# Attention stage of a hybrid decoder layer: dividing by the row sums before the transposes, short blocks in a second PSUM place, a new order in the unit, mean squares token-major

## What is computed

```python
logits = jnp.einsum('bqhd,bkhd->bhqk', q_blk, k) * scale + (c_q[..., :, None] - c_k[:, :, None, :])
p = jax.nn.softmax(jnp.where(causal, logits, -jnp.inf), axis=-1)
return jnp.einsum('bhqk,bkhd->bqhd', p, v)
...
mix = jnp.concatenate([_rmsnorm(rec, rec_out_norm_w[l]), _rmsnorm(att, attn_out_norm_w[l])], axis=-1)
x = x + jnp.einsum('bse,ed->bsd', mix, w_out[l])
```

## Time and profile before

| what | value |
|---|---|
| median of 3 runs | 2045.23 us (2040.22 to 2046.78) |
| the profiled execution | 2041.34 us, of which the span is 2039.6 us |
| PE busy | 1899.4 us (93% of the span) |
| DVE busy | 1277.3 us (63%) |
| ACT busy | 1050.6 us (52%) |
| stage B, first score work to last norm work | about 284 to 450 us of the span |
| stage C | 450.3 to about 568 us |

### The profile page before, as it was taken

One profiled execution on the slowest core, in us unless ns is written; L12 is line 12 of the kernel. 1 busy time (PEld: TensorE's weight loads), 2 busy tenths in 40 slices (PEclk: granted clock), 3 DMA queues, 4 the chain that ended last, 5 costly groups with the idle time before them and its releaser, 6 DMA issues.

```text
span 2039.6 us, 51127 instructions
## 1 busy us (share of the span) xinstructions
PE 1899.4 (93%) x20629; PEld 1761.9 (86%) x20629; DVE 1277.3 (63%) x2642; ACT 1050.6 (52%) x1442; POOL 402.3 (20%) x302
## 2 busy tenths in 40 slices
PE   6999988979968999999999999999999999989982
PEld 4777756658858999999999999999999999988982
DVE  4543647764378555566665567776677687776681
ACT  5574335552105444455555556555665665655661
POOL 4010000001002111111111112213243243333241
PEclk9999999989968999999999999999999999999996
DMA  4111010015377788889999899999999999999994
GB/s 141 52 42 42 21 62 1 2 46 189 137 260 246 262 280 280 272 274 304 306 306 306 303 310 312 312 327 336 371 354 372 371 353 371 370 351 369 369 346 114
DMA packets 251771, 501.81 MB, mean 246 GB/s; under 512 B 13025, under 2 KB 33809, under 8 KB 251585
## 3 DMA queue, kind: packets, MB, share of 16 engines
q1 hardware_dynamic: 231376, 446.73, 60.4%
q0 software_dynamic: 20256, 51.73, 11.7%
q10 hardware_dynamic: 48, 2.10, 0.3%
HBM read 471.16 MB, written 52.43 MB: 257 GB/s over the span
## 4 chain that ended last, share of the span: by engine, by line
PE 54%; DVE 4%; DMA 4%; issue 4%; SPq 2%; ACT 1%; POOL 0%; DVEq 0%; ACTq 0%; POOLq 0%
PE E_p_d L1945 22%; PE E_p_g L1934 5%; PE E_p_g L1937 5%; PE E_p_g L1936 5%; PE E_p_u L1937 5%; PE E_p_u L1934 5%; PE E_p_u L1936 5%; DMA E_w_st<-in_w_down 4%; DVE E_w_lo L1775 3%; SPq L1570 2%; PE E_p_t L1916 2%; PE E_p_t L1901 2%; ACT E_w_hi L1689 1%; DVE E_up L1835 0%; DVE E_gate L1823 0%
## 5 line engine op out<-in xcount | busy, mean ns | idle before, releaser
L1775 DVE SCALAR_TENSOR_TENSOR E_w_lo<-E_w_st,E_w_hi 128x2048 f16<-128x2048 f32 x260 | 594.8, 2288 | 60.3 <-ACT E_w_hi L1689 56.6
L1689 ACT ACTIVATE E_w_hi<-E_w_st 128x2048 f16<-128x2048 f32 x260 | 493.0, 1906 | 142.4 <-PE E_p_g L1937 95.7
L1945 PE MATMUL E_p_d<-E_a_f,E_w_st 128*128 128x160 f32 (+6 forms) x4096 | 536.3, 291 | 21.7 <-DMA E_w_st<-in_w_down 13.4
L1945 PEld LDWEIGHTS E_p_d<-E_a_f,E_w_st 128*128 128x128 f32 x4096 | 521.2, 193 | 29.2 <-DMA E_w_st<-in_w_down 16.2
L1934 PE MATMUL E_p_g<-E_x_hi,E_w_hi 128*128 128x160 f16 (+6 forms) x2048 | 373.0, 224 | 7.2 <-DVE E_w_lo L1775 7.2
L1934 PE MATMUL E_p_u<-E_x_hi,E_w_hi 128*128 128x160 f16 (+6 forms) x2048 | 371.7, 223 | 5.0 <-DVE E_w_lo L1775 5.0
L1936 PE MATMUL E_p_g<-E_x_lo,E_w_hi 128*128 128x160 f16 (+6 forms) x2048 | 373.0, 224 | 0.0
L1937 PE MATMUL E_p_g<-E_x_hi,E_w_lo 128*128 128x160 f16 (+6 forms) x2048 | 372.9, 224 | 0.0
L1937 PE MATMUL E_p_u<-E_x_hi,E_w_lo 128*128 128x160 f16 (+6 forms) x2048 | 371.6, 223 | 0.0
L1936 PE MATMUL E_p_u<-E_x_lo,E_w_hi 128*128 128x160 f16 (+6 forms) x2048 | 371.6, 223 | 0.0
L1633 POOL DMA_INDIRECT sum_rows<-E_y_rows,E_idx_out x66 | 169.0, 2561 | 596.6 <-ACT E_y_rows L1707 586.4
(11 more groups left out here) (375 smaller groups left out, 2758.7 us busy)
## 6 DMA issues: line engine op xcount, KB each, us to landing
E_w_st<-in_w_gate_up SPq DMA_DIRECT2D x130, 2048.0 KB, 15.7
E_w_st<-in_w_down SPq DMA_DIRECT2D x64, 2048.0 KB
A_w_st<-in_w_in SPq DMA_DIRECT2D x20, 512.0 KB, 3.9
sum_rows<-C_x SPq DMA_DIRECT2D x10, 512.0 KB, 5.8
A_x_rows<-in_x SPq DMA_DIRECT2D x8, 512.0 KB, 8.2
...
```

The lines of the kernel that those rows point to most:

```text
L1689: act.activation(w_hi[c % RI][:], staged(c % NG), ACT.Copy, scale=SW).then_inc(hi_s, 1)
L1775: dve.scalar_tensor_tensor(out=w_lo[c % RI][:], in0=staged(c % NG), scalar=SW, in1=w_hi[c % RI][:], op0=ALU.mult, op1=ALU.subtract, accum_ ...
L1945: ins = pe.matmul(banks[:, h, 0:w], staged(c)[:, k, h * P:(h + 1) * P], x[:, k, 0:w], start=h == 0 and k == 0, stop=k == KT - 1, skip_grou ...
```

## The change

Stage B: once two exponentials' sums are there, DVE takes two reciprocals (`inverse(n)`), and the score tile itself is scaled before it is turned (`normal`): tile n on DVE, tiles n+1, n+2 and n+3 on ACT. The spreading matmuls and the multiplication of `out_rows` are gone. Tiles n+2 and n+3 are turned into `p_o[1]` instead of `p_t`. PE's order becomes: wide scores, turn n, weigh(u-1, short), turn n+2, turn n+1, slim scores, turn n+3, (sums), weigh(u, long). ACT and DVE keep their tiles in an order that fits. `sums` now has the squares as the fixed operand and one column of ones as the moving one, so that the means stand one per partition; eight matmuls of one column, written to two columns of `p_s[0]`. The reciprocal of all means is taken once, over 128x8.

Stage C: the root is taken of 128x8 after the second of the four splits of rec; eight matmuls between `rec_part(0)` and `rec_part(1)` spread it over the partitions into PSUM, and DVE's scaling reads it there.

```diff
+        def home_of(n):
+            return p_o[1] if n % 4 >= 2 else p_t
...
             def turn(n):
-                pe.wait_ge(exp_s, n + 1)
+                if n % 4:
+                    pe.wait_ge(norm_act, 3 * (n // 4) + n % 4)
                 else:
+                    pe.wait_ge(norm_dve, n // 4 + 1)
+                u, e = n // 4, n % 4
+                if e == 0 and u:
+                    pe.wait_ge(turn_dve, 2 * u - 1)
+                elif e == 1:
+                    pe.wait_ge(turn_act, 2 * u + 1)
+                elif e == 2 and u:
+                    pe.wait_ge(turn_dve, 2 * u)
+                elif e == 3:
+                    pe.wait_ge(turn_act, 2 * u + 2)
...
             def weigh(u, side):
-                pe.wait_ge(inv_s, u + 1)
-                if u:
-                    pe.wait_ge(out_s, 2 * u - 1 + side)
-                for e in range(2):
-                    pe.matmul(p_o[0][e * HD:(e + 1) * HD, o + P:o + 2 * P],
-                              row_inv[:, n + e:n + e + 1].to_broadcast([P, HD]), m.ident[:], start=True, stop=True)
+                if u or side:
+                    pe.wait_ge(out_s, 2 * u + side)
...
             def sums(q):
-                for c in range(CT):
-                    ins = pe.matmul(p_o[1][:, 0:2 * P], m.rec_ones[:], square[:, c, :], start=c == 0, stop=c == CT - 1)
+                for side in range(2):
+                    for c in range(CT):
+                        ins = pe.matmul(p_s[0][:, 512 + side:513 + side], square[:, c, side * P:(side + 1) * P],
+                                        m.rec_ones[:, 0:1], start=c == 0, stop=c == CT - 1, skip_group_check=True)
...
@@ tensor: body of unit u
                 if u:
                     weigh(u - 1, 1)
+                turn(n + 2)
                 turn(n + 1)
                 if u + 1 < NU:
                     score_pair(n + 6)
-                turn(n + 2)
-                weigh(u, 0)
                 turn(n + 3)
                 if u % 4 == 1 and u > 4:
                     sums(u // 4 - 1)
+                weigh(u, 0)
@@ scalar: body of unit u
+            def normal(n):
+                act.wait_ge(inv_s, 2 * (n // 4) + 1 + n % 4 // 2)
+                act.activation(tile_of(n)[:, 0:L], tile_of(n)[:, 0:L], ACT.Copy, scale=row_inv[:, n:n + 1]
+                               ).then_inc(norm_act, 1)
+                normal(n + 2)
+                normal(n + 3)
                 keep_turned(n)
+                keep_turned(n + 2)
                 if u + 1 < NU:
                     exps(n + 4)
                     exps(n + 5)
-                keep_turned(n + 2)
-                if u + 1 < NU:
                     exps(n + 6)
                     exps(n + 7)
+                    normal(n + 5)
@@ vector: body of unit u
-                inverse(u)
+                inverse(n + 2)
...
                     subtract(n + 6)
                     subtract(n + 7)
+                    inverse(n + 4)
+                    normal(n + 4)
+                keep_turned(n + 3)
+                if u % 4 == 1 and u > 4:
+                    mean(u // 4 - 1)
                 out_rows(u, 0)
-                keep_turned(n + 3)
...
+            dve.wait_ge(ms_s, T // 2)
+            step(dve.reciprocal(m.att_ms[:], m.att_ms[:]))
@@ stage C
-            act.activation(att_rs[:], m.att_ms[:], ACT.Sqrt).then_inc(att_ok, 1)
+                if g == 1:
+                    act.activation(att_rs[:], m.att_ms[:], ACT.Sqrt).then_inc(att_ok, 1)
...
             rec_part(0)
+            pe.wait_ge(att_ok, 1)
+            for t in range(T):
+                ins = pe.matmul(p_m[t // 4][:, t % 4 * P:(t % 4 + 1) * P], att_rs[:, t:t + 1].to_broadcast([P, P]), m.ident[:],
+                                start=True, stop=True)
+                if t % 4 == 3:
+                    ins.then_inc(rs_mm, 1)
```

More of the change, by code:

```diff
@@ L745, in rows_of, with out_at, turned_no @@
             return slice(i * P, (i + 1) * P)
+        def out_at(side):
+            return 2 * P * side
+        def home_of(n):
+            return p_o[1] if n % 4 >= 2 else p_t
+        def turned_no(n):
+            return n - n % 4 + (1, 3, 2, 4)[n % 4]
         BY_DVE = {0: 1, 4: 2, 6: 3}
@@ L783, in score_pair @@
                     pe.wait_ge(score_s, n)
+                u = n // 4
+                if n % 4 == 0 and u % 4 == 3 and u > 4:
+                    pe.wait_ge(ms_s, (u - 2) // 4)
                 for c0 in range(0, L, 512):
@@ L949, in keep_turned, with inverse, normal @@
                 L = P * (where(n)[0] + 1)
[L950 removed]
+                dve.wait_ge(turn_mm, turned_no(n))
                 if n >= 4:
                     dve.wait_ge(pv_mm, 2 * (n // 4) - 1 + n % 4 // 2)
[L953 to L957 removed]
+                dve.tensor_copy(turned_of(n)[:, 0:L], home_of(n)[:, 0:L]).then_inc(turn_dve, 1)
+            def inverse(n):
+                dve.wait_ge(exp_s, n + 2)
+                dve.reciprocal(row_inv[:, n:n + 2], m.row_sum[:, n:n + 2]).then_inc(inv_s, 1)
+            def normal(n):
+                L = P * (where(n)[0] + 1)
+                dve.wait_ge(inv_s, 2 * (n // 4) + 1)
+                dve.tensor_scalar(tile_of(n)[:, 0:L], tile_of(n)[:, 0:L], row_inv[:, n:n + 1], None,
+                                  ALU.mult).then_inc(norm_dve, 1)
             def out_rows(u, side):
[L960 removed]
+                o = out_at(side)
                 dve.wait_ge(pv_mm, 2 * u + 1 + side)
[L962 to L965 removed]
+                dve.tensor_copy(m.att[:, u % 4, rows_of(u // 4, side)], p_o[0][:, o:o + P]).then_inc(out_s, 1)
             def mean(q):
@@ L969, in mean @@
                 for side in range(2):
-                    ins = dve.tensor_scalar(m.att_ms[:, rows_of(q, side)], p_o[1][:, side * P:(side + 1) * P], EPS, None,
-                                            ALU.add)
+                    i = blocks[q][side]
+                    ins = dve.tensor_scalar(m.att_ms[:, i:i + 1], p_s[0][:, 512 + side:513 + side], EPS, None, ALU.add)
                 ins.then_inc(ms_s, 1)
-                dve.wait_ge(ms_s, q + 1)
-                for side in range(2):
-                    step(dve.reciprocal(m.att_ms[:, rows_of(q, side)], m.att_ms[:, rows_of(q, side)]))
             key_rows(0)
@@ L983, in _ @@
             key_rows(6)
+            inverse(0)
+            normal(0)
             for u in range(NU):
                 n = 4 * u
-                inverse(u)
+                inverse(n + 2)
                 if u + 1 < NU:
@@ L1002, in _ @@
                                       ALU.subtract).then_inc(wo_lo_s, 1)
-                if u % 4 == 1 and u > 4:
-                    mean(u // 4 - 1)
             out_rows(NU - 1, 1)
             mean(T // 2 - 1)
+            dve.wait_ge(ms_s, T // 2)
+            step(dve.reciprocal(m.att_ms[:], m.att_ms[:]))
 def stage_c(nc, m, a):
@@ L1133, in _ @@
                 dve.tensor_tensor(mix_lo[:, c, :], m.rec[:, c, :], f32(mix_hi[:, c, :]), ALU.subtract).then_inc(mix_lo_s, 1)
[L1134 removed]
             for half in range(2):
                 r = slice(half * 512, (half + 1) * 512)
+                dve.wait_ge(rs_mm, half + 1)
                 for c in range(CT):
                     dve.scalar_tensor_tensor(out=m.att[:, c, r], in0=m.att[:, c, r], scalar=att_w[:, c:c + 1],
[L1139 removed]
+                                             in1=p_m[half][:], op0=ALU.mult, op1=ALU.mult).then_inc(att_n, 1)
                 if half == 0:
```

43 lines of the change are left out of this document (15 added, 28 removed).

## The result

| | median | range | runs |
|---|---|---|---|
| before | 2044.31 us | 2040.22 to 2046.78 | 6 |
| changed | 2032.61 us | 2029.18 to 2035.38 | 6 |

The ratio is 0.9944, 95% interval 0.9930 to 0.9959: 11.7 us faster, between 8.4 and 14.3. The prediction was 2036.6 us, in a range of 2028 to 2044. The profiled execution took 2033.14 us (span 2031.4), 8.2 less than that of before.

A forecast was written before the change was run, and what follows sets the result against it. Stage B was taken to be paced by a ring of waits with no engine full, stage C's main part by PE. From 2045.2 us, -15.0 + 7.0 - 4.6 + 4.0 = -8.6 gave 2036.6 us, range 2028 to 2044.

The forecast's parts named there:

- The signs it named: Stage B and C: foretold body times, `wo_lo` waiting in bodies 3, 7, 11, last result about 10 us earlier.
- two signs that were to mean failure as a whole: PE's clock in the loop below 1.00, or divisions taking longer than the rows they are priced by.
- Term 1, the ring: Stage B loop: short turns move into waits and spreadings go, shortening the ring of waits; -15.0 us.
- Term 2, the divisions' side effects: Stage B: divisions make `wo_hi`, `wo_lo`, the second reciprocal and ACT's first copy late; +7.0 us.
- slower: the clock: Rival: PE's new stalls lower its clock in stage B's late bodies, 1.8 us each; ten give 2055; chance 0.07.
- Term 3, the tail: End of stage B: shorter last body, one multiply gone, reciprocals of 1.94 us become one of 128x8; -4.6 us.
- The sums between them I cost equal: End of stage B: the last sums, between final multiply and reciprocals, were to cost the same as before.
- Term 4, stage C: Start of stage C: root and spreading delay DVE's scaling, so `att_part(0)` comes 4.0 us late; +4.0 us.
- the upper end of the prediction: Start of stage C: cost of 6 us if PE's stalls keep the low clock longer.
- The sums' price: Stage B, bodies 5, 9, 13: sixteen records at 0.114 us each, 1.8 us in all.

The follow-up runs named there:

- e_best: The change with second reciprocal ahead of `wo_lo`, `wo_hi` ahead of the wide division, and stage C's spreading earlier; 2022.65 us, 0.9907 of the kernel before.
- e_ms: The kernel before with only the change's new mean squares, and stage C as in the change; 2039.60 us, 0.9983 of the kernel before.
- r_after: The change once more without an edit, also called the repeat; 2032.07 us, 0.9957 of the kernel before.
- e_both: The change with two edits: second reciprocal ahead of `wo_lo`, and `wo_hi` ahead of the wide division; 2026.05 us, 0.9922 of the kernel before.
- e_spread: The change with stage C's spreading moved earlier, after PE's second group of three matmuls of tile 0; 2026.45 us, 0.9927 of the kernel before.
- e_place2: The kernel before plus new mean squares, division first and second turning place, old order, `mean` ahead of `wo_lo`; 2040.39 us, 0.9989 of the kernel before.
- e_divboth: The kernel before plus new mean squares and division, one turning place, old order, reciprocal ahead of `wo_lo`, `wo_hi` ahead of wide division; 2031.98 us, 0.9958.
- e_hi: The change with ACT doing `wo_hi` ahead of the wide division; 2027.73 us, 0.9933 of the kernel before.

## Why the prediction was right

**The signs it named.** Body 2 took 8.16 us (8.5 foretold), body 6 7.51 (7.8), body 5 9.18 (9.4), body 8 9.00 (over 9), and `wo_lo` waited 1.2 to 1.3 in bodies 3, 7 and 11. The last result came 6.1 earlier, and 10.1 counted from the start of body 0 (10 foretold). But two signs that were to mean failure as a whole also came. PE's clock in the loop was below 1.00: 0.97 over the fourteen bodies, 0.99 in the repeat (the kernel before had 0.98 over its fourteen). And ACT's divisions took longer than their price, 1.14 us for 1024 columns and 0.39 for 128, for 1.04 and 0.3. The time came out in spite of both, since the low clock struck one or two bodies, and 0.1 us a division is small beside waits of a microsecond.

**Term 1, the ring (-15.0).** `e_best` is the change with the side effects out, `e_ms` supplies bodies 0 and 1 of the old loop at full clock. Between them: bodies 0 to 3 lose 0.80, 0.82, 0.90 and 0.89 (predicted 0.8 each); bodies 4 and 6 1.06 and 1.07 (1.0), body 7 0.32 (1.0, since `wo_lo` still stands there); bodies 8, 10, 11 together 2.2 (2.7); body 12 0.85 (0.3); bodies 5, 9, 13 together 4.5 (5.8). Sum 13.4. The links were right, and what looks missing in body 13 (0.7 for 1.8) is mostly what term 2 booked there for ACT's squares, 0.8. With the squares (0.6 and 0.8) the prediction had 13.6 for what is measured here. The timeline of the changed kernel, body 13:

```profile
411.97 1.13 ACT L915 ACTIVATE B_square<-att 128x512 f32<-128x512 f32 x2
...
413.76 0.66 PE L827 MATMUL B_p_o<-ident,B_slim 128*128 128x128 f32 x4 [0.23 <-ACT B_slim L900]
...
415.06 0.74 PE L827 MATMUL B_p_t<-ident,B_wide 128*128 128x128 f32 x5 [0.63 <-ACT B_probs_t L908]
...
417.35 1.84 PE L851 MATMUL B_p_s<-rec_ones,B_square 128*128 128x1 f32 x16
```

PE waits 0.86 us behind ACT's squares and divisions and is busy for the other 9.1, where the prediction had 8.9 of work.

**Term 2, the divisions' side effects (+7.0).** The bodies of the change less those of `e_best`: 7.0 us in the first execution, 6.0 in the repeat. The squares are in both kernels of this difference, so the 5.6 that the prediction had without them is what stands beside it. By the medians the two edits are worth 6.0 (`r_after` to `e_both`) and 3.8 (`e_spread` to `e_best`). The chain of waits is the one described, and the bodies fit in part: bodies 3, 7 and 11 carry 0.8 to 0.9 each, which the prediction booked to the body behind them (4, 8, 12). What it put down to plain waiting in bodies 8 and 12 (1.9, 2.3) is to a good part the granted clock: PE waited 1.9 us in body 8, and then its work ran at 0.50. That is the mechanism of the rival "slower: the clock", at about the price it named (1.8 us a body; measured 2.1 in body 8, of which the waits and the clock are not told apart). It came in one or two bodies, not in the nine that the rival needed. So this term has the right size with a cause in it that the prediction had turned down; that is luck in part.

The Trainium skill ("TensorE: Matmul & The Clock Gate", Part 1) ties the clock to how busy PE is. The runs agree in this: with the division and neither of the two edits body 8 had the low clock in five of six profiled executions, and with one or both edits in none of six. How much waiting it takes no run shows: body 12 of the repeat and body 8 of `e_place2` stayed at 1.00 behind the waits that went with the low clock elsewhere. The prediction let the trace decide against that rule because the loop of before held 1.00 through its own stalls. It took body 1 for the price of a low clock and did not ask what stood ahead of it there. The timeline of the kernel before, body 1, has the same two waits as body 2 in the earlier trace rows, and the low clock behind them:

```profile
307.66 1.06 PE L806 MATMUL B_p_t<-ident,B_wide 128*128 128x128 f32 x8 [0.62 <-ACT B_probs_t L885]
...
310.20 0.30 PE L806 MATMUL B_p_t<-ident,B_slim 128*128 128x128 f32 x1 [0.83 <-DVE B_probs_t L953]
...
310.91 3.33 PE L825 MATMUL B_p_o<-B_probs_t,v 128*64 128x128 f32 x32
```

The same multiply takes 1.94 in body 2. Why the clock fell in the one body and not in the other stays open.

**Term 3, the tail (-4.6).** Tail -1.5 where -2.4 was predicted; last copy to stage C -3.9 where -2.2 was. The last body took 7.53 us from its first turn and not 6.5. The reciprocals gave 1.9 as worked out (`e_ms`: -1.96 for this stretch, with the sums at the low clock as before). "The sums between them I cost equal" failed: 1.96 us near full clock (0.96) for 3.49 near the low one (0.56). The prediction had priced the form and not the clock. The gap ahead of the sums is 1.56 us here and was 1.89.

**Term 4, stage C (+4.0).** 3.6 in the first execution, 4.9 in the repeat, and 3.6 to 5.9 in the eight experiments with the same start of stage C. The four executions above 4.5 (`r_after`, `e_both`, `e_divboth`, `e_hi`) have a mean clock of 0.62 to 0.68 over the first 15 us of the stage, the others 0.77 to 0.81, so the spread goes with the clock, as the upper end of the prediction had it. The chain went step by step as told: table load, spreading behind the first part, DVE's scaling waiting 4.69 us for it and starting 5.25 later in the stage than before, `att_part(0)` waiting for L1148's successor L1181. `e_spread` shows that the cost hangs on the spreading's place in PE's queue. The extra that the Trainium skill gives a PSUM operand ("VectorE: DVE Perf Modes", the errata section) doesn't show: four scalings take 2.72 us from PSUM and 2.74 from SBUF.

**Sum.** Like for like the profiles give -13.4 + 7.0 (or 6.0) - 5.4 + 3.6 (or 4.9), so -7.9 to -8.2, against -8.6 predicted. The two measurements say -11.7 and -9 (0.9957). The rest is within their intervals, and the profiles offer no further cause that belongs to the change. That the sum of the profiles comes so near is luck in part: the tail gave 0.9 less than told, and the clock in the last sums 1.5 more. The sums' price of 0.115 us a record held (1.84 for sixteen). The floor of about 25 ns that the Trainium skill gives between small matmuls ("TensorE: Matmul & The Clock Gate", Part 1) is a lower bound; taken for the price it would have given 0.4, which these records are far above.
